# Expert gates: weighted one-hot rows by one compare-and-multiply per token, three of four tokens on GpSimd

## The chip, the cores and the metric

One core of a Trainium2 chip. The metric is the device time of one execution in microseconds (us); smaller is better. All data is fp32.

## The reference

A network of two parts: two layers with feed-forward, Fourier and retention mixers, then two layers (DEPTH = 2) with attention, a recurrent mixer and a product-key expert layer, all for 256 tokens of width 1024. The change lies in the expert layer, which is once in each of the last two layers. It has 128 x 128 experts; each token picks 16 of them in each of 8 heads:

```python
def block(zb):
    q = (zb @ wq).reshape(PEER_TOK_BLOCK, Hp, 2, half)
    s = jnp.einsum('thpd,hpnd->thpn', q, subkeys).astype(jnp.float32)
    s_top, i_top = lax.top_k(s, K)
    cand = (s_top[:, :, 0, :, None] + s_top[:, :, 1, None, :]).reshape(PEER_TOK_BLOCK, Hp, K * K)
    score, flat = lax.top_k(cand, K)
    i1 = jnp.take_along_axis(i_top[:, :, 0], flat // K, axis=-1)
    i2 = jnp.take_along_axis(i_top[:, :, 1], flat % K, axis=-1)
    expert = i1 * PEER_NKEYS + i2
    gate = jax.nn.softmax(score, axis=-1)
    h = jnp.einsum('thkd,td->thk', u_tab[expert], zb).astype(jnp.float32)
    act = (gate * jax.nn.gelu(h, approximate=False)).astype(zb.dtype)
    return jnp.einsum('thk,thkd->td', act, v_tab[expert])
```

The kernel gathers no expert. It runs all of them for all tokens and multiplies by a dense table of gates, which holds for token t the gate at (i1, i2), and zero where an expert wasn't picked.

## The kernel before, in words

**Stages.** The program is a list of stages, and each of the engines (TensorE or PE, VectorE or DVE, ScalarE or ACT, GpSimd or POOL, SyncE or SP) runs its part of them in this order; a stage begins where the semaphore `stage_done` has reached its index. Weights come in blocks of 1 MB through a ring of four (SP issues the loads). ScalarE rounds each block and POOL subtracts the rounded block from the whole one (line 269), so that PE can work with both parts.

**The stage of the gates** is `PeerGates` (lines 2667 to 2731), between `PeerRoute`, which picks the experts, and `PeerExperts`, which runs them. `PeerRoute` leaves in `slot` three rows for each of 256 tokens: i1, i2 and the gate, with the 8 x 16 = 128 picks along the partitions. For one token the gate table of 128 x 128 is then a product over the picks: (one-hot rows of i1, each times its gate) transposed, times (one-hot rows of i2).

- The tokens go in 64 sets (`SETS`) of four (`SET`). `hot` holds four sets (`BUFS`), each with two halves of four 128x128 rows; half 0 is for i1 and half 1 for i2.
- DVE copies iota (0 to 127) into PSUM (line 2693), so that its second input comes from there. For each set it compares iota with i1 and i2 of the four tokens in one instruction of 1024 elements (line 2698) and signals `hot_ready`. From the fifth set on it waits for `done` of the set four before.
- POOL waits for `hot_ready` and multiplies half 0 by the gates in place, 512 elements (line 2707), then signals `weighted`.
- PE waits for `weighted` and, from the fourth set on, for `kept` of the set three before, then does four products of 128x128 (line 2717), two records each, into one of three PSUM banks, and signals `done`.
- ScalarE copies each bank of 512 to the table (line 2728) and signals `kept`. After the last it ends the stage (line 2731).

**Around it.** At the stage's start ScalarE may round blocks that the experts need (line 2723) and waits for earlier stores (line 2724). POOL's queue goes from the last set straight into `PeerExperts.pool`, which makes the remainders of its first blocks (line 269), and DVE's into line 2918. The experts on PE begin at line 2797. The order on each engine is that of the program text; there is no planner.

Of the kernel before, what the change touches and what calls it, by code (L numbers as in the profile page):

```python
# [11 lines left out]
ALU = mybir.AluOpType  # L12
AX = mybir.AxisListType

P = 128
# [63 lines left out]
def columns(table, name, layer=0, width=None):  # L79
    a, b = VEC[name]  # L80
    if width is None:
        return table[:, a:b]
    return table[:, a + layer * width:a + (layer + 1) * width]
# [18 lines left out]
class Share:  # L102
# [3 lines left out]
    def at(self, k):  # L106

        return self.base + k
# [80 lines left out]
class Stage:  # L189
# [82 lines left out]
    def pe(self, pe):  # L272
        pass
# [4 lines left out]
    def dve(self, dve, link):  # L278
        pass
# [62 lines left out]
class Modulation:  # L342
# [5 lines left out]
    TILE = 32  # L348
    SETS = 4
    LATER = 2  # L350
# [43 lines left out]
    def block(self, pe, i):  # L394
# [9 lines left out]
        for e in range(steps):  # L404
            k = steps * (i - 8 * n) + e
            for g in range(self.SETS):
                at = (e * self.SETS + g) * width
                last = mm(c.ps[g * self.TILE:(g + 1) * self.TILE, self.BANK + n % 2, 0:width], self.cond[:, k, :],  # L408
# [25 lines left out]
    def add(self, dve, link, n):  # L434
# [4 lines left out]
        m = self.mods[:].rearrange("p j d s -> p (j d) s")[:, 16 * n:16 * n + 4 * tiles, :].rearrange("p (g m) s -> p g m s", m=tiles)  # L439
        turned = c.ps[:, self.TURNED, 32 * n:32 * n + 8 * tiles].rearrange("p (m g s) -> p g m s", g=self.SETS, s=2)  # L440
        b = columns(c.vec, "b_mod", self.layer, 72)[:, 16 * n:16 * n + 4 * tiles].rearrange("p (g m) -> p g m", m=tiles)
        link(v.tensor_tensor(m, turned, b.unsqueeze(3).broadcast_to([P, self.SETS, tiles, 2]), ALU.add))
        for j in range(2 * n, min(2 * n + 2, N_MOD)):
# [14 lines left out]
class Norm(Stage):  # L458
# [86 lines left out]
    def pe(self, pe):  # L545
# [15 lines left out]
        if self.first_mods:  # L561
# [4 lines left out]
            lead.turn(pe, 0)  # L566

    def dve(self, dve, link):
        c, nc = self.chip, self.nc
        if self.first_mods:  # L570
# [855 lines left out]
class Attention(Stage):  # L1426
# [10 lines left out]
    CMP, SEL, WIN, SWA = range(4)  # L1437
    BUFS = 4
    LEAD = 3
    units = [(t, g, b) for t in range(NT) for g in range(2) for b in range(4)]  # L1440

    def __init__(self, chip, layer, tables):
# [16 lines left out]
        n += 16 + P  # L1459
        assert n + self.BUFS * 8 * 4 <= W_PEND  # L1460
        self.stat = at(n, self.BUFS, 8, 4)
        self.sc = at(B_WORK, self.BUFS, 4, N)
        n = B_WORK + self.BUFS * 4 * N
        self.pt = at(n, 5, 4, P)
# [25 lines left out]
    def pe(self, pe):  # L1490
# [51 lines left out]
        def turn(u):  # L1542
# [5 lines left out]
            for j in range(self.key_tiles(t, b)):  # L1548
                for i in range(4):
                    last = nc.tensor.transpose(ps[0:w, 4 + j, i * P:(i + 1) * P], self.sc[:, u % self.BUFS, i, j * P:j * P + w],  # L1550
                                               self.chip.ident)
# [1115 lines left out]
class PeerGates(Stage):  # L2667
# [4 lines left out]

    SET = 4
    SETS = N // SET
    BUFS = 4
    BANKS = 3

    def __init__(self, chip):
# [5 lines left out]
        self.iota_kept = chip.signals("iota_in_psum", 1)  # L2684
        self.hot_ready = chip.signals("hot_ready", self.SETS)
        self.weighted = chip.signals("weighted", self.SETS)
        self.done = chip.signals("gates_done", self.SETS)
        self.kept = chip.signals("gates_kept", self.SETS)

    def dve(self, dve, link):  # L2690
        v, wide = self.nc.vector, [P, 2, self.SET, P]
        dve.wait_ge(self.chip.stage_done, self.index)
        v.tensor_copy(self.iota, self.chip.iota).then_inc(self.iota_kept.sem, 1)
        dve.wait_ge(self.iota_kept.sem, self.iota_kept.at(1))
        for n in range(self.SETS):
            if n >= self.BUFS:
                dve.wait_ge(self.done.sem, self.done.at(n - self.BUFS + 1))
            v.tensor_tensor(self.hot[:, n % self.BUFS], self.iota.unsqueeze(1).unsqueeze(1).broadcast_to(wide),
                            self.slot[:, 0:2, n * self.SET:(n + 1) * self.SET].unsqueeze(3).broadcast_to(wide),
                            ALU.is_equal).then_inc(self.hot_ready.sem, 1)  # L2700

    def pool(self, pool, link):
        pool.wait_ge(self.chip.stage_done, self.index)
        for n in range(self.SETS):
            hot = self.hot[:, n % self.BUFS, 0]
            pool.wait_ge(self.hot_ready.sem, self.hot_ready.at(n + 1))
            self.nc.gpsimd.tensor_tensor(hot, hot, self.slot[:, 2, n * self.SET:(n + 1) * self.SET].unsqueeze(2)
                                         .broadcast_to([P, self.SET, P]), ALU.mult).then_inc(self.weighted.sem, 1)

    def pe(self, pe):  # L2710
        pe.wait_ge(self.chip.stage_done, self.index)
        for n in range(self.SETS):
            pe.wait_ge(self.weighted.sem, self.weighted.at(n + 1))
            if n >= self.BANKS:
                pe.wait_ge(self.kept.sem, self.kept.at(n - self.BANKS + 1))
            for i in range(self.SET):
                last = self.nc.tensor.matmul(self.chip.ps[:, n % self.BANKS, i * P:(i + 1) * P], self.hot[:, n % self.BUFS, 0, i],  # L2717
                                             self.hot[:, n % self.BUFS, 1, i], start=True, stop=True)
            last.then_inc(self.done.sem, 1)
# [603 lines left out]
```

## Time and profile before

| | |
|---|---|
| median of 3 runs | 4693.72 us (4690.62 to 4700.74) |
| the profiled execution | 4701.88 us |
| its span, first to last instruction | 4700.1 us |
| busy, share of the span | PE 94%, PEld (weight loads) 80%, POOL 56%, ACT 38%, DVE 35% |
| mean granted clock of TensorE | 0.969 |

The stage of the gates runs twice, from about 2560 to 2637 us and from about 3939 to 4015 us. The profile names an instruction by its line, engine and operation, then output<-input with their shapes as partitions x elements; `arena` is the big SBUF buffer that holds `hot`, `slot` and the gates, `ps` is PSUM. Times are of one execution, so a sum is made against the 4701.88 us and then carried to the median.

### The profile page before, as it was taken

The page shows a single profiled execution, that of the slowest core. Times are in us where ns is not written, and L with a number is a line of the kernel's source. Part 1 is how long each engine was busy: PE and PEld are TensorE (multiplying, and loading weights), DVE is VectorE, ACT ScalarE, POOL GpSimd, SP SyncE. Part 2 cuts the span into 40 slices and gives each one's busy share as a digit, 9 for nine tenths or more (in the row PEclk, how much of TensorE's full clock was granted, in tenths as well). Part 3 has the DMA queues.
Part 4 walks back from the last instruction along what each step waited for, and adds up shares of the span by engine and source line. Part 5 has one row for each costly group of instructions (what it writes and reads, how often), then busy time and mean ns, then how long its engine had stood idle before and what let it go on. Part 6 is the DMA issues. An engine that isn't in the chain of part 4 may idle for free.

```text
span 4700.1 us, 62596 instructions
## 1 busy us (share of the span) xinstructions
PE 4437.7 (94%) x24682; PEld 3755.9 (80%) x24682; DVE 1650.6 (35%) x3195; ACT 1806.1 (38%) x2932; POOL 2641.5 (56%) x1282
## 2 busy tenths in 40 slices
PE   7999999999999989889989999999898989999998
PEld 5777777778778879886888888887877888888886
DVE  2211222032010532264468522223454568322223
ACT  3222322132233234434232555555442333555554
POOL 3343243344444357651166888888640366888886
PEclk9999999999999999999999999999999999999999
DMA  6622366222232234440134255555440143355554
GB/s 258 242 106 90 70 247 235 85 90 99 90 107 91 81 117 171 175 171 28 37 144 139 90 187 187 187 187 202 166 153 19 67 143 101 139 187 188 187 187 161
DMA packets 100139, 659.22 MB, mean 140 GB/s; under 512 B 10464, under 2 KB 16864, under 8 KB 22368
## 3 DMA queue, kind: packets, MB, share of 16 engines
q1 hardware_dynamic: 90000, 638.46, 37.6%
q10 hardware_dynamic: 9936, 17.86, 1.4%
q8 instruction: 151, 2.47, 0.2%
q14 instruction: 52, 0.43, 0.0%
HBM read 646.84 MB, written 9.44 MB: 140 GB/s over the span
## 4 chain that ended last, share of the span: by engine, by line
PE 86%; DVE 7%; ACT 2%; POOL 2%; issue 1%; DMA 1%; SPq 0%; ACTq 0%; DVEq 0%; POOLq 0%
PE ps L2807 14%; PE ps L253 14%; PE ps L254 13%; PE ps L255 13%; PE ps L2797 8%; PE ps L2798 4%; PE ps L2717 3%; PE ps L2513 3%; PE ps L1399 2%; POOL ring_rest L269 2%; PE ps L408 1%; PE ps L1569 1%; PE ps L1538 1%; DVE arena L2235 1%; PE ps L1903 1%
## 5 line engine op out<-in xcount | busy, mean ns | idle before, releaser
L269 POOL TENSOR_TENSOR ring_rest<-ring,rounded 128x1024 fp32r<-128x1024 f32 x960 | 2346.4, 2459 | 1489.4 <-ACT rounded L241 1290.8
L253 PE MATMUL ps<-part,rounded 128*128 128x256 f32 (+1 forms) x3456 | 1188.4, 344 | 84.1 <-DVE part L2343 22.4
L254 PE MATMUL ps<-part,rounded 128*128 128x256 f32 (+1 forms) x3456 | 1176.8, 341 | 0.0
L255 PE MATMUL ps<-part,ring_rest 128*128 128x256 f32 (+1 forms) x3456 | 1175.1, 340 | 0.0
L253 PEld LDWEIGHTS ps<-part,rounded 128*128 128x128 f32 x3456 | 670.7, 194 | 186.4 <-issue 26.7
L241 ACT ACTIVATE rounded<-ring 128x1024 fp32r<-128x1024 f32 x496 | 496.4, 1050 | 689.1 <-PE ps L255 679.3
L255 PEld LDWEIGHTS ps<-part,ring_rest 128*128 128x128 f32 x3456 | 670.4, 194 | 69.0
L254 PEld LDWEIGHTS ps<-part,rounded 128*128 128x128 f32 x3456 | 671.3, 194 | 67.4
L2797 PE MATMUL ps<-x_parts,rounded 128*128 128x512 f32 x1728 | 616.9, 397 | 1.5 <-ACTq L2731 1.5
L2896 ACT ACTIVATE rounded<-ring 128x1024 fp32r<-128x1024 f32 x464 | 490.3, 1057 | 329.1 <-DMA ring<-in_weights 327.0
L2807 PE MATMUL ps<-rounded,part 128*128 128x512 f32 x2048 | 592.4, 393 | 16.6 <-POOL ring_rest L269 10.0
L2798 PE MATMUL ps<-x_parts,ring_rest 128*128 128x256 f32 x1728 | 484.7, 280 | 0.0
L2807 PEld LDWEIGHTS ps<-rounded,part 128*128 128x128 f32 x2048 | 368.9, 188 | 99.6 <-POOL ring_rest L269 13.4
L2797 PEld LDWEIGHTS ps<-x_parts,rounded 128*128 128x128 f32 x1728 | 324.6, 188 | 79.4 <-ACTq L2731 1.8
L2798 PEld LDWEIGHTS ps<-x_parts,ring_rest 128*128 128x128 f32 x1728 | 325.9, 189 | 8.3
L2927 DVE TENSOR_TENSOR ps<-ps,arena 128x256 f32<-128x256 f32 x216 | 134.8, 624 | 545.6 <-ACT ps L2864 545.6
L2807 PE MATMUL ps<-ring_rest,part 128*128 128x512 f32 x1024 | 320.6, 395 | 0.0
L686 ACT ACTIVATE arena<-ps 128x512 f32<-128x512 f32 (+1 forms) x88 | 47.9, 544 | 617.8 <-PE ps L255 617.8
L700 DVE TENSOR_TENSOR part<-ps,arena 128x512 f32<-128x512 f32 (+1 forms) x88 | 55.0, 625 | 556.9 <-ACT arena L686 556.9
L2807 PEld LDWEIGHTS ps<-ring_rest,part 128*128 128x128 f32 x1024 | 192.1, 188 | 47.3
L772 DVE SCALAR_TENSOR_TENSOR x<-ps,mods,x 128x256 f32<-128x256 f32 x80 | 35.8, 480 | 507.1 <-PE ps L255 507.1
L2321 POOL TENSOR_TENSOR part<-arena,part 128x1024 fp32r<-128x1024 f32 x6 | 14.5, 2423 | 304.0 <-ACT part L2301 304.0
(362 smaller groups left out, 5374.8 us busy)
## 6 DMA issues: line engine op xcount, KB each, us to landing
ring<-in_weights SPq DMA_DIRECT2D x528, 1024.0 KB, 4.8
arena<-in_mod_weights SPq DMA_DIRECT2D x72, 1024.0 KB, 7.9
held<-arena ACTq DMA_DIRECT2D x20, 256.0 KB, 5.5
arena<-held SPq DMA_DIRECT2D x20, 256.0 KB, 4.5
arena<-bias_scratch ACTq DMA_DIRECT2D x2, 2048.0 KB, 9.9
bias_scratch<-arena ACTq DMA_DIRECT2D x1, 3072.0 KB, 32.1
x<-in_x SPq DMA_DIRECT2D x1, 2048.0 KB, 9.9
arena<-in_keys ACTq DMA_DIRECT2D x2, 1024.0 KB, 4.8
```

The costliest lines, as they stand in the source:

```text
L241: self.nc.scalar.activation(c.rounded[:, s % ROUNDED, half], c.ring[:, slot, half], ACT.Copy)\
L253: mm(out, w[0], a[0], start=start, stop=False)
L254: mm(out, w[0], a[1], start=False, stop=False)
L255: return mm(out, w[1], a[0], start=False, stop=stop)
L269: eng.tensor_tensor(c.ring_rest[:, slot, half], c.ring[:, slot, half], c.rounded[:, (self.s0 + r) % ROUNDED, half].bitcast(F32), ALU.subtr ...
L2513: last = nc.tensor.matmul(ps[:, 4 + u % self.AHEAD_BANKS, 0:N], self.chip.ring[:, slot, e * KD + k, :], self.z_whole[:, k, :], start=k == ...
L2717: last = self.nc.tensor.matmul(self.chip.ps[:, n % self.BANKS, i * P:(i + 1) * P], self.hot[:, n % self.BUFS, 0, i], self.hot[:, n % self. ...
L2797: nc.tensor.matmul(c.ps[:, r % 2, :], whi[:, k, :], c.x_parts[:, k, :], start=k == 0, stop=False)
L2798: last = nc.tensor.matmul(c.ps[:, r % 2, 0:N], wlo[:, k, :], self.z[0][:, k, :], start=False, stop=k == KD - 1)
L2807: last = nc.tensor.matmul(self.out(t, i), a, w[:, i * 4 * P:(i + 1) * 4 * P], start=False, stop=end and n == 2)
L2896: self.nc.scalar.activation(c.rounded[:, (self.s0 + r) % ROUNDED, half], c.ring[:, f % RING, half], ACT.Copy)\
L2927: v.tensor_tensor(gelu, gelu, self.gates[:, :, bass.ds(b + HELD, 1)].rearrange("p t a -> p (t a)"), ALU.mult)\
```

## The change

The multiplication by the gate and the comparison with i1 become one instruction per token: `tensor_scalar` with iota as its input and two column operands (one value per partition each), i1 for `is_equal` and the gate for `mult`. POOL does it for three tokens of each set (`OWN`), reading iota from SBUF, and no longer waits for DVE; from the fifth set on it waits for `done` as DVE does. DVE compares i2 for all four tokens (512 elements) and does the fused instruction for the fourth token, reading iota from PSUM. PE waits for both.

```diff
@@ -2672,6 +2672,7 @@
 
     SET = 4
     SETS = N // SET
+    OWN = 3
     BUFS = 4
     BANKS = 3
 
@@ -2687,29 +2688,38 @@
         self.done = chip.signals("gates_done", self.SETS)
         self.kept = chip.signals("gates_kept", self.SETS)
 
+    def weigh(self, eng, iota, n, i):
+        token = n * self.SET + i
+        return eng.tensor_scalar(self.hot[:, n % self.BUFS, 0, i], iota, self.slot[:, 0, token:token + 1],
+                                 self.slot[:, 2, token:token + 1], ALU.is_equal, ALU.mult)
+
     def dve(self, dve, link):
-        v, wide = self.nc.vector, [P, 2, self.SET, P]
+        v, wide = self.nc.vector, [P, self.SET, P]
         dve.wait_ge(self.chip.stage_done, self.index)
         v.tensor_copy(self.iota, self.chip.iota).then_inc(self.iota_kept.sem, 1)
         dve.wait_ge(self.iota_kept.sem, self.iota_kept.at(1))
         for n in range(self.SETS):
             if n >= self.BUFS:
                 dve.wait_ge(self.done.sem, self.done.at(n - self.BUFS + 1))
-            v.tensor_tensor(self.hot[:, n % self.BUFS], self.iota.unsqueeze(1).unsqueeze(1).broadcast_to(wide),
-                            self.slot[:, 0:2, n * self.SET:(n + 1) * self.SET].unsqueeze(3).broadcast_to(wide),
-                            ALU.is_equal).then_inc(self.hot_ready.sem, 1)
+            v.tensor_tensor(self.hot[:, n % self.BUFS, 1], self.iota.unsqueeze(1).broadcast_to(wide),
+                            self.slot[:, 1, n * self.SET:(n + 1) * self.SET].unsqueeze(2).broadcast_to(wide), ALU.is_equal)
+            for i in range(self.OWN, self.SET):
+                last = self.weigh(v, self.iota, n, i)
+            last.then_inc(self.hot_ready.sem, 1)
 
     def pool(self, pool, link):
         pool.wait_ge(self.chip.stage_done, self.index)
         for n in range(self.SETS):
-            hot = self.hot[:, n % self.BUFS, 0]
-            pool.wait_ge(self.hot_ready.sem, self.hot_ready.at(n + 1))
-            self.nc.gpsimd.tensor_tensor(hot, hot, self.slot[:, 2, n * self.SET:(n + 1) * self.SET].unsqueeze(2)
-                                         .broadcast_to([P, self.SET, P]), ALU.mult).then_inc(self.weighted.sem, 1)
+            if n >= self.BUFS:
+                pool.wait_ge(self.done.sem, self.done.at(n - self.BUFS + 1))
+            for i in range(self.OWN):
+                last = self.weigh(self.nc.gpsimd, self.chip.iota, n, i)
+            last.then_inc(self.weighted.sem, 1)
 
     def pe(self, pe):
         pe.wait_ge(self.chip.stage_done, self.index)
         for n in range(self.SETS):
+            pe.wait_ge(self.hot_ready.sem, self.hot_ready.at(n + 1))
             pe.wait_ge(self.weighted.sem, self.weighted.at(n + 1))
             if n >= self.BANKS:
                 pe.wait_ge(self.kept.sem, self.kept.at(n - self.BANKS + 1))
```

## Rows read from the trace of the kernel before

**Rows 1.** The page, part 4: the chain that ended last

```profile
PE ps L2807 14%; PE ps L253 14%; PE ps L254 13%; PE ps L255 13%; PE ps L2797 8%; PE ps L2798 4%; PE ps L2717 3%; PE ps L2513 3%; PE ps L1399 2%; POOL ring_rest L269 2%; PE ps L408 1%; PE ps L1569 1%; PE ps L1538 1%; DVE arena L2235 1%; PE ps L1903 1%
```

**Rows 2.** The chain of waits, 2555 to 2650 us; start us, us, what

```profile
2559.66 0.31 DVE ps L2693
2559.99 1.24 DVE arena L2698
...
2561.36 1.05 POOL arena L2707
...
2562.54 73.72 PE ps L2717 x512
2636.28 0.61 ACT arena L2728
2636.98 0.50 PE ps L2797
```

**Rows 3.** Lines from 2574 to 2635 us: busy us, mean ns, idle before

```profile
L2717 PE MATMUL ps<-arena 128*128 128x128 f32 x433 | 61.4, 288 | 0.0
L2698 DVE TENSOR_TENSOR arena<-ps,arena 128x1024 f32<-128x1024 f32 x53 | 60.0, 1210 | 0.0
L2707 POOL TENSOR_TENSOR arena<-arena 128x512 f32<-128x512 f32 x54 | 56.2, 1041 | 4.9
L2717 PEld LDWEIGHTS ps<-arena 128*128 128x128 f32 x432 | 52.3, 191 | 8.8 <-POOL arena L2707 8.8
```

**Rows 4.** Timeline from 2568 us; start us, us, engine line, [idle before, releaser]

```profile
2568.04 8.18 DVE L2698 TENSOR_TENSOR arena<-ps,arena 128x1024 f32<-128x1024 f32 x7 [0.48 <-PE ps L2717]
...
2570.24 0.60 ACT L2728 ACTIVATE arena<-ps 128x512 f32<-128x512 f32 x1 [0.30 <-PE ps L2717]
...
2571.13 0.60 ACT L2728 ACTIVATE arena<-ps 128x512 f32<-128x512 f32 x1 [0.30 <-PE ps L2717]
2572.02 0.60 ACT L2728 ACTIVATE arena<-ps 128x512 f32<-128x512 f32 x1 [0.30 <-PE ps L2717]
...
2574.00 0.97 PEld L2717 LDWEIGHTS ps<-arena 128*128 128x128 f32 x8 [0.16 <-POOL arena L2707]
```

**Rows 5.** Windows by engine, core 0; fifth pair of columns POOL, then PEclk

```profile
2562.50:2568.00 5.50, 5.46 (x25) 5.49 (x26) 4.55 (x4) 1.19 (x2) 4.45 (x5) 0.50 0.00 0
...
2574.00:2635.00 61.00, 61.00 (x433) 52.25 (x432) 59.91 (x53) 32.27 (x54) 56.20 (x55) 1.00 0.01 1
```

**Rows 6.** L2698 over both layers; duration min/median/max ns, first and last start

```profile
L2698 DVE TENSOR_TENSOR arena<-ps,arena x128: 1210/1210/1225, 2560.0 to 4010.5; 128x1024 f32<-128x1024 f32 x128
```

**Rows 7.** Lines by form, engine DVE: one input, none to two column operands

```profile
L2134 DVE TENSOR_SCALAR arena<-arena,vec 128x128 f32<-128x128 f32 x16 | 4.5, 342 | 0.1
...
L2124 DVE TENSOR_SCALAR arena<-ps 128x512 f32<-128x512 f32 x4 | 2.8, 691 | 15.0 <-PE ps L1855 14.9
...
L1837 DVE TENSOR_SCALAR x<-arena,vec 128x256 f32<-128x256 f32 x8 | 2.3, 349 | 0.1
...
L2071 DVE TENSOR_SCALAR arena<-arena 128x1024 f32<-128x1024 f32 x2 | 1.4, 694 | 18.1 <-ACT arena L1990 18.1
```

**Rows 8.** Timeline of DVE at 2308 us: four of those back to back

```profile
2308.78 1.11 DVE L2134 TENSOR_SCALAR arena<-arena,vec 128x128 f32<-128x128 f32 x4
```

**Rows 9.** Lines by form, engine POOL, whole span

```profile
L1720 POOL TENSOR_TENSOR arena<-arena 128x1024 f32<-128x1024 f32 x12 | 22.7, 1894 | 40.1 <-DVE arena L1704 38.7 <-DVE arena L1699 1.4
...
L1720 POOL TENSOR_TENSOR arena<-arena 128x512 f32<-128x512 f32 x12 | 12.5, 1041 | 34.0 <-DVE arena L1704 23.2 <-DVE arena L1699 10.8
...
L2584 POOL TENSOR_TENSOR arena<-arena 128x32 f32<-128x32 f32 x32 | 7.1, 243 | 1.3
L2580 POOL TENSOR_TENSOR arena<-arena 128x128 f32<-128x128 f32 x16 | 6.4, 401 | 1.3
```

**Rows 10.** Timeline of POOL near 3920 us: two instructions back to back

```profile
3924.75 0.44 POOL L2584 TENSOR_TENSOR arena<-arena 128x32 f32<-128x32 f32 x2
```

**Rows 11.** L2614: min/median/max ns of one form

```profile
L2614 DVE TENSOR_TENSOR arena<-arena x16: 268/268/2483, 2450.2 to 3908.8; 128x112 f32<-128x112 f32 x16
```

## The prediction

> **What bounds the kernel now.** I read the page's chain first, to see what the touched code can be worth. TensorE carries the run, and the one-hot products of line 2717 hold 3% of the chain, some 150 us in two layers [rows 1]. So only this stage moves, and the rest of the 4.7 ms stays as it is. The chain of waits through the first layer's stage puts it in order: DVE copies iota at 2559.66, compares set 0, GpSimd multiplies it, and from 2562.54 the chain stays on PE for 73.72 us until ScalarE's last copy; 0.09 us after that copy the experts begin at 2636.98 [rows 2]. A chain on PE isn't yet a stage bound by PE, so the next views ask who paces it.
>
> In the middle of the stage DVE is busy for 60.0 us in 53 comparisons with no idle time, that is 1.132 us a set (the single instruction reads 1210 ns; neighbours overlap by 78). POOL has 4.9 us of idle time in 54 sets. PE's weight loads stand 8.8 us waiting for POOL, about 0.16 us in every set [rows 3]. PE shows as fully busy only because its ends are modelled. DVE is the pace, POOL (1.04 us a set) comes right behind it, PE behind both. How fast PE would go is seen where it eats sets that were made ahead: ScalarE's copies then start at 2570.24, 2571.13 and 2572.02, 0.89 us apart, and the weight loads wait for POOL again at 2574.00 [rows 4]. Earlier, from 2562.5 to 2568, PE has granted clock 0.50 (1.2 GHz) after its pause, and later 1.00 (2.4 GHz) [rows 5]; in that slow stretch PE is the bound whatever the makers do. In layer 1 DVE works without a break from 2568.04, with 58 of 64 sets to come [rows 4]; in layer 2 it is free of the slow stretch sooner and goes at its own pace for all 64 [rows 6]. So 122 sets are paced by the maker.
>
> **The change, part by part.** The new pace P is the slowest of three: DVE, POOL, PE.
>
> DVE loses half of its comparison: 512 elements in place of 1024. A one-input operation on 512 elements from PSUM takes 691 ns [rows 7], against 1210 for the 1024 [rows 3]: 519 ns less (1.014 ns an element), so the cadence is 1.132 - 0.519 = 0.61 us. It gains one compare-and-multiply of 128 elements from PSUM with two column operands. The nearest row is line 2134: two column operands, 128 elements, 342 ns, and four of them in 1.11 us, so one every (1.11 - 0.342)/3 = 0.256 us [rows 7, 8]. That row reads SBUF, where 1024 elements cost (694 ns) what 512 cost from PSUM (691): half the price per element. From PSUM it is 128 x 0.507 = 0.065 us more, 0.32 us. DVE: 0.61 + 0.32 = 0.93 us.
>
> POOL loses a 128x512 product (1041 ns) and gains three compare-and-multiplies of 128x128 a set, 384 in both layers. No POOL row shows that operation, so its price is the unknown of this change. POOL's two-input rows lie on a line: (1894 - 1041)/512 = 1.67 ns an element and 188 ns fixed, which gives 401 for 128 elements, as measured [rows 9]. Two of them back to back take 0.44 us where one takes 0.243, so 46 ns of each is hidden [rows 10]. The new one has one input in place of two: at best 0.83 ns an element, 107 ns; at worst the rate stays, 213 ns. It also fetches two columns. On DVE the rows without, with one and with two of them have fixed parts of 694 - 519 = 175, 349 - 130 = 219 and 342 - 65 = 277 ns [rows 7]: 44 for one, 102 for both. For POOL the ends are then 188 + 107 = 295 ns (columns free) and 188 + 213 + 102 = 503 ns. I take the halved element price, since it is the second stream that goes, and 73 ns for the columns, between one fetch and two: 368 ns, 322 in a row. Three are 0.97 us.
>
> The GPSIMD Engine Reference of the Trainium skill (section 4.1) calls one-input operations on GpSimd roughly line-rate, which agrees with the halved slope; no POOL row here shows one. The same page (section 7) says that a loop that produces a truth value costs about 2.03 cycles an element unless it is unrolled, and that each small read command costs about 102 cycles. By estimates from these the operation would be near 295 ns or near 570 ns, which is P at 0.93 or at 1.57, and the stage faster than DVE's old pace or much slower.
>
> PE keeps its products and gets a second wait a set: 0.89 us and at most the 0.16 us of its present handover again, 1.05 [rows 4]. I take it as hidden: both makers run ahead of it and the 0.97 of POOL covers 0.08 us. ScalarE's copies follow PE as before.
>
> So P = 0.97, and the steady part gains 122 x (1.132 - 0.97) = 19.8 us.
>
> The ends: POOL no longer stands behind DVE. The first product could start at 2559.66 + 0.33 + 0.61 + 0.32 + 0.08 + 0.13 = 2561.1 in place of 2562.54 [rows 2]: 1.4 us. At the end a product of 1.04 us with its handover is off the chain: 1.2 us. In layer 1 both count (makers and PE are tied together in the slow stretch), in layer 2 the makers' chain is one piece and 1.5 us is left: 4.1 us. Against it: some operations of DVE now and then take some 2.2 us more than their kind, as line 2614 with 268 ns at the median and 2483 at most [rows 11]. A new form at the start can meet that on either engine: 0 to 2.2 us a layer, taken as 1: 2 us. The buffers, of which there are still four, the waits for free ones and the queues of SP and ScalarE are unchanged. POOL's next work, two remainders of the first expert block, starts when its last set is done, and so moves with the stage.
>
> Sum: 19.8 + 4.1 - 2 = 21.9 us. The profiled execution took 4701.9 us, so 4680 by its own time; the median of the three runs is 4693.7, 0.17% lower, and the forecast against it is 4672.
>
> One more way to lose: DVE and GpSimd share a way into SBUF. The rows show no such loss (POOL's product reads 1041 ns in line 1720 and beside DVE's comparisons alike [rows 3, 9]). SBUF — State Buffer of the Trainium skill ("Who interferes with whom") says that a `tensor_scalar` in a two-port mode shuts GpSimd out for its whole length; were it so, POOL's pace would be 0.97 + 0.32 = 1.29. Its condition is a source in SBUF, and the copy of iota in PSUM stays the source on DVE, so I leave this out of the sum and give it 0.02 of the chance of slower.
>
> **The rivals.** With POOL's operation at d ns, P = 3(d - 46), and the whole changes sign at P = 1.149, d = 429.
>
> *Slower, POOL becomes the bound.* The element price doesn't fall: d = 188 + 213 + 73 = 474, P = 1.28, 122 x (-0.15) + 2 = -16 us, 4710; with both columns at full price d = 503, P = 1.37, -29 us with the 2.2 us starts, 4723. Dearer still, if each column took half of POOL's fixed 188 ns: d = 589, P = 1.63, -59 us, 4752; this is where the skill's two costs of section 7 point, and it has 0.08 of the 0.32. For it: three fixed parts of 188 ns stand in place of one, 0.42 us a set more, and POOL was already at 92% of its pace. Against it: one stream goes.
>
> *No change.* d between 403 and 455, P 1.07 to 1.23: the plain two-input row of 401 ns is at the edge of it. 4684 to 4703.
>
> *All of it is realised.* d up to 356: DVE at 0.93 is the bound, with PE right behind. 122 x 0.20 + 4.1 = 28.7 us without the start cost: 4665. This is the better end of my own case. If the second wait costs PE its full 0.16, P = 1.05 and the gain 12 us, 4682, still my case.
>
> **How the numbers follow.** A change under 0.2% (9.4 us) can't be told from none. My case, d below 403 ns, runs from 4665 to 4684 and gets 0.52 (0.22 of it at the DVE bound); no change 0.16; slower 0.32. The range takes in the best end with 2 us of play, 4663, and the slower case up to 4723 with as much play as the runs before show (7 us), 4730; the dearer 0.08 is left out, with some 0.05 below.
>
> **What would show it.** In the profile after: three POOL TENSOR_SCALAR rows a set, 128x128, near 368 ns (right: under 403; wrong: over 455); DVE's comparison near 691 ns and its small one near 400; POOL without idle time in the stage, PE's weight loads waiting for POOL; ScalarE's copies 0.97 us apart; the stage about 63 us long instead of 74. If they are 0.93 apart and wait for DVE, the better end holds; over 1.15 apart, the forecast is wrong and POOL's price is the step that failed. A wait of PE that ends with neither maker would say that its second wait costs.

## The result, and the profile after

The changed kernel takes 4852.1 us (median of 4 runs, 4849.5 to 4854.5) against 4696.6 us before: ratio 1.033, 95% interval 1.0315 to 1.0346. It is some 155 us slower, where a gain of 22 us was forecast and 4730 was the upper end.

The page of the changed kernel, cut to its span, its busy times and the clock in 40 slices:

```profile
span 4847.7 us, 62984 instructions
...
PE 4504.4 (93%) x24682; PEld 3813.2 (79%) x24682; DVE 1636.7 (34%) x3323; ACT 1805.3 (37%) x2932; POOL 2803.4 (58%) x1538
...
PEclk9999999999999999999997899999999997899999
```

POOL has 162 us more busy time than before. The clock row has two dips, in the 22nd and 23rd and in the 34th and 35th of its 40 slices; they hold the two stages of the gates. The new operation over the whole run, on both engines (duration min/median/max in ns):

```profile
L2693 POOL TENSOR_SCALAR arena<-cst,arena x384: 790/834/875, 2556.0 to 4155.1; 128x128 f32<-128x128 f32 x192
L2693 DVE TENSOR_SCALAR arena<-ps,arena x128: 399/402/405, 2556.9 to 4148.6; 128x128 f32<-128x128 f32 x128
```

DVE, with iota in PSUM, does it in 402 ns and GpSimd, with iota in SBUF, in 834. The groups in the middle of the stage, which answer to [rows 3] (busy us, mean ns, idle before):

```profile
L2693 POOL TENSOR_SCALAR arena<-cst,arena 128x128 f32<-128x128 f32 x150 | 116.1, 829 | 0.0
L2727 PE MATMUL ps<-arena 128*128 128x128 f32 x400 | 80.9, 366 | 35.1 <-DVE arena L2693 23.8 <-issue 11.2
L2727 PEld LDWEIGHTS ps<-arena 128*128 128x128 f32 x399 | 70.2, 265 | 45.0 <-DVE arena L2693 27.1 <-issue 17.9
L2704 DVE TENSOR_TENSOR arena<-ps,arena 128x512 f32<-128x512 f32 x50 | 34.6, 692 | 64.7 <-PE ps L2727 64.7
L2738 ACT ACTIVATE arena<-ps 128x512 f32<-128x512 f32 x50 | 29.9, 597 | 85.3 <-PE ps L2727 85.3
L2693 DVE TENSOR_SCALAR arena<-ps,arena 128x128 f32<-128x128 f32 x50 | 20.1, 402 | 0.0
```

POOL has no idle time at all in 115 us. Before, it was idle 4.9 us in 61. DVE, the pace before, now waits 64.7 us for TensorE's `done`, and ScalarE 85.3 us. This reads as one engine that paces everybody. The timeline of the same stretch shows one period, of 2.32 us:

```profile
2599.32 13.19 POOL L2693 TENSOR_SCALAR arena<-cst,arena 128x128 f32<-128x128 f32 x17
...
2600.24 2.05 PE L2727 MATMUL ps<-arena 128*128 128x128 f32 x8 [1.19 <-DVE arena L2693]
2602.32 0.60 ACT L2738 ACTIVATE arena<-ps 128x512 f32<-128x512 f32 x1 [2.64 <-PE ps L2727]
2602.32 0.69 DVE L2704 TENSOR_TENSOR arena<-ps,arena 128x512 f32<-128x512 f32 x1 [2.23 <-PE ps L2727]
...
2604.64 0.60 ACT L2738 ACTIVATE arena<-ps 128x512 f32<-128x512 f32 x1 [1.72 <-PE ps L2727]
```

POOL does 17 operations in 13.19 us without a gap. The releaser that PE names here is DVE's small operation, and the groups above name it too. The start of the stage shows that this is not what PE waited for, and it has the prices of DVE's two operations back to back:

```profile
2557.56 23.23 POOL L2693 TENSOR_SCALAR arena<-cst,arena 128x128 f32<-128x128 f32 x30
...
2558.11 0.68 DVE L2704 TENSOR_TENSOR arena<-ps,arena 128x512 f32<-128x512 f32 x1
...
2558.50 2.04 PE L2727 MATMUL ps<-arena 128*128 128x128 f32 x8 [3.06 <-POOL arena L2693]
2558.71 0.40 DVE L2693 TENSOR_SCALAR arena<-ps,arena 128x128 f32<-128x128 f32 x1
2559.03 0.68 DVE L2704 TENSOR_TENSOR arena<-ps,arena 128x512 f32<-128x512 f32 x1
2559.62 0.41 DVE L2693 TENSOR_SCALAR arena<-ps,arena 128x128 f32<-128x128 f32 x1
...
2564.91 0.40 DVE L2693 TENSOR_SCALAR arena<-ps,arena 128x128 f32<-128x128 f32 x1
...
2565.41 1.78 PE L2727 MATMUL ps<-arena 128*128 128x128 f32 x8 [1.15 <-DVE arena L2693]
```

POOL's 30 operations take 23.23 us: 0.774 us from one start to the next, 2.32 a set. PE's row at 2565.41 is the fourth set. DVE had made its rows for that set by 2560.03 (the pair at 2559.03 and 2559.62); the operation at 2564.91, which the profile names, is for the seventh. POOL's twelfth operation, the last of the fourth set, ends near 2556.01 + 12 x 0.774 = 2565.30, and PE starts 0.11 us later. DVE runs three sets ahead, ScalarE and DVE wait for PE, PE waits for POOL, and POOL never waits.

From 2558.11 to 2558.71 and on to 2559.03 are 0.60 and 0.32 us, together 0.92 where 0.93 was forecast. DVE's copy of iota, with which the stage starts, begins at 2555.94 in this run, and the first product comes 2.56 us later, where it took 2.88 before [rows 2].

### The profile page after: what moved, and what is told of

Read it like the earlier page. It is cut to its first block, busy times and chain, and to the rows that moved or that the text cites. A ratio compares the mean times of both kernels' runs of the same rounds, so it can differ in the third digit from the quotient of the medians.

```text
span 4847.7 us, 62984 instructions
## 1 busy us (share of the span) xinstructions
PE 4504.4 (93%) x24682; PEld 3813.2 (79%) x24682; DVE 1636.7 (34%) x3323; ACT 1805.3 (37%) x2932; POOL 2803.4 (58%) x1538
## 4 chain that ended last, share of the span: by engine, by line
PE 85%; DVE 8%; ACT 2%; issue 2%; POOL 2%; DMA 1%; SPq 0%; ACTq 0%; DVEq 0%; POOLq 0%
PE ps L2817 14%; PE ps L253 13%; PE ps L254 13%; PE ps L255 13%; PE ps L2807 8%; PE ps L2727 4%; PE ps L2808 4%; PE ps L2513 3%; PE ps L1399 2%; POOL ring_rest L269 2%; PE ps L408 1%; PE ps L1538 1%; PE ps L1569 1%; DVE arena L2235 1%; PE ps L1903 1%
## 5 line engine op out<-in xcount | busy, mean ns | idle before, releaser
L2693 POOL TENSOR_SCALAR arena<-cst,arena 128x128 f32<-128x128 f32 x384 | 297.1, 830 | 19.3 <-ACTq L2565 19.3
L2727 PE MATMUL ps<-arena 128*128 128x128 f32 x1024 | 213.4, 374 | 89.2 <-DVE arena L2693 52.4
L2727 PEld LDWEIGHTS ps<-arena 128*128 128x128 f32 x1024 | 186.0, 273 | 116.8 <-DVE arena L2693 59.5
```

The lines of the kernel that those rows point to most:

```text
L2693: return eng.tensor_scalar(self.hot[:, n % self.BUFS, 0, i], iota, self.slot[:, 0, token:token + 1], self.slot[:, 2, token:token + 1], ALU ...
```

## The experiments

All were made from the changed kernel by editing GpSimd's operation alone, if nothing else is said. "In a row" is the time from one start to the next, read from a timeline row as its length over its count. The total of the kernel before, in the same jobs, was between 4690 and 4702 us. Every version but the last was run once, so the readings rest on the traces more than on the totals.

### One column in place of two

```diff
@@ -2692,0 +2693,3 @@
+        if eng is self.nc.gpsimd:
+            return eng.tensor_scalar(self.hot[:, n % self.BUFS, 0, i], iota, self.slot[:, 0, token:token + 1],
+                                     1.0, ALU.is_equal, ALU.mult)
```

> On GpSimd the gate's column is replaced by the constant 1.0 (so the gate is left out for three of four tokens); all else as in the changed kernel, where one operation costs 0.774 us in a row. Theory F (the fetches of the two columns are the price): one fetch gone, (0.774 - 0.25)/2 = 0.26 us less an operation, pace 2.32 -> about 1.54 us a set, total about 4752. Theory E (the price is per element, in the loop) and theory C (the comparison takes a slow path): no change, pace 2.32, about 4852.

Measured 4817.4 us, between the two. POOL in the timeline from 2575 us:

```profile
2574.75 15.29 POOL L2694 TENSOR_SCALAR arena<-cst,arena 128x128 f32<-128x128 f32 x22
```

15.29/22 = 0.695 us in a row. The column is worth 0.08 us, not 0.26: theory F falls as the main cause.

### No column

```diff
@@ -2692,0 +2693,2 @@
+        if eng is self.nc.gpsimd:
+            return eng.tensor_scalar(self.hot[:, n % self.BUFS, 0, i], iota, 5.0, 1.0, ALU.is_equal, ALU.mult)
```

> Both columns on GpSimd are constants (5.0 and 1.0; the one-hot rows of three of four tokens are left out of the computation). Theory F: the operation falls to about 0.25 us in a row, POOL is no longer the bound, DVE's pace of 0.93 holds, about 4670. Theories E and C: pace 2.32, about 4852.

Measured 4818.4 us, nearer to theories E and C. POOL's group from 2575 to 2650 us:

```profile
L2694 POOL TENSOR_SCALAR arena<-cst 128x128 f32<-128x128 f32 x106 | 68.1, 642 | 7.2
```

The operation itself is shorter again (642 ns against 721 with one column), but POOL now has 7.2 us of idle time over 106 operations with no releaser named, and the time from one to the next is (68.1 + 7.2)/106 = 0.71 us, no better than with one column. So with both columns gone nine tenths of the price are still there.

### No comparison

```diff
@@ -2692,0 +2693,3 @@
+        if eng is self.nc.gpsimd:
+            return eng.tensor_scalar(self.hot[:, n % self.BUFS, 0, i], iota, self.slot[:, 0, token:token + 1],
+                                     self.slot[:, 2, token:token + 1], ALU.mult, ALU.mult)
```

> On GpSimd the comparison is replaced by a multiplication, with both columns kept (the one-hot of three of four tokens is left out). Theory C: the operation loses its slow path and falls to 0.25 to 0.37 us in a row, pace 0.93 to 1.1, total 4670 to 4690. Theories F and E: no change, pace 2.32, about 4852.

Measured 4712.0 us, 22 us above the upper end of theory C and 140 below the others. POOL in the timeline from 2575 us:

```profile
2574.91 15.43 POOL L2694 TENSOR_SCALAR arena<-cst,arena 128x128 f32<-128x128 f32 x36
```

15.43/36 = 0.429 us in a row, 0.345 less than with the comparison, where theory C had 0.25 to 0.37 us. Both columns, the second multiplication, the input and the places are the same; only the first operation differs. It is the comparison.

### Two halves

```diff
@@ -2692,0 +2693,6 @@
+        if eng is self.nc.gpsimd:
+            for h in range(0, P, P // 2):
+                last = eng.tensor_scalar(self.hot[:, n % self.BUFS, 0, i, h:h + P // 2], iota[:, h:h + P // 2],
+                                         self.slot[:, 0, token:token + 1], self.slot[:, 2, token:token + 1],
+                                         ALU.is_equal, ALU.mult)
+            return last
```

> Each of GpSimd's operations is made as two, of 64 elements each: six in place of three a set, the same elements. Theory F (a fixed price, paid per instruction): 0.72 us each, pace about 4.3, total about 5105. Theory E (188 ns fixed less 46 hidden, the rest 4.9 ns an element): 0.14 + 64 x 0.0049 = 0.46 us each, pace 2.75, total about 4907. Theory C as E, if the slow path is in the loop.

Measured 4978.1 us, between the two, so neither was right as it stood. POOL in the timeline from 2575 us:

```profile
2574.46 16.08 POOL L2695 TENSOR_SCALAR arena<-cst,arena 128x64 f32<-128x64 f32 x29
```

16.08/29 = 0.555 us for 64 elements against 0.774 for 128: 3.42 ns an element, and 0.336 us that does not depend on them, if the two lengths lie on a straight line; no third length was tried.

### Only the comparison

```diff
@@ -2692,0 +2693,3 @@
+        if eng is self.nc.gpsimd:
+            return eng.tensor_scalar(self.hot[:, n % self.BUFS, 0, i], iota, self.slot[:, 0, token:token + 1],
+                                     None, ALU.is_equal)
```

> GpSimd only compares: one column and one stage of arithmetic, no multiplication (the gate is left out for three of four tokens). The runs so far: both columns and comparison 0.774 us in a row, one column and a constant about 0.70, two columns with a multiplication in place of the comparison 0.43. Theory K (a comparison costs about 2.7 ns an element more in GpSimd's loop, wherever it stands): about 0.65 to 0.70 us, pace 2.0 to 2.1, total 4800 to 4817. Rival S (it is the comparison's result fed to a second stage that is slow): 0.33 to 0.40 us, pace about 1.1, total 4690 to 4710.

Measured 4771.8 us, between the theories, nearer to K. POOL in the timeline from 2575 us:

```profile
2574.66 15.61 POOL L2694 TENSOR_SCALAR arena<-cst,arena 128x128 f32<-128x128 f32 x27
```

15.61/27 = 0.578 us. Without any second stage the comparison is still 0.15 us dearer than two multiplications with two columns. The second stage with its constant is worth 0.12 of the 0.695; rival S, by which the second stage makes the whole difference, falls. A lone multiplication was not run, so how the 0.345 us would come out without a second stage is not known.

### Two tokens for GpSimd, two for DVE

```diff
@@ -2675 +2675 @@
-    OWN = 3
+    OWN = 2
```

> GpSimd weighs two of four tokens, DVE the other two. If the stage is simply paced by the slower maker: POOL 2 x 0.774 = 1.55 us a set, DVE 0.61 + 2 x 0.32 = 1.25; 128 x 0.774 = 99 us less than the changed kernel and a few more for the clock that TensorE gets back, about 4748. Rival (DVE and GpSimd stand in each other's way once both are busy): POOL's operation above 0.8 us in a row, total above 4760.

Measured 4746.5 us against 4748 expected. POOL in the timeline from 2575 us:

```profile
2574.91 15.49 POOL L2693 TENSOR_SCALAR arena<-cst,arena 128x128 f32<-128x128 f32 x20
```

15.49/20 = 0.775 us, unchanged while DVE, which has the other two tokens, is idle for only 6.2 of 45 us. The two engines don't hold each other up here, and the count of operations times 0.774 is the pace.

### Each product twice

```diff
@@ -2727,2 +2727,3 @@
-                last = self.nc.tensor.matmul(self.chip.ps[:, n % self.BANKS, i * P:(i + 1) * P], self.hot[:, n % self.BUFS, 0, i],
-                                             self.hot[:, n % self.BUFS, 1, i], start=True, stop=True)
+                for again in range(2):
+                    last = self.nc.tensor.matmul(self.chip.ps[:, n % self.BANKS, i * P:(i + 1) * P], self.hot[:, n % self.BUFS, 0, i],
+                                                 self.hot[:, n % self.BUFS, 1, i], start=True, stop=True)
```

> The changed kernel with each of TensorE's gate products made twice over into the same place, so that it works through its idle time (the same result). POOL's pace of 2.32 us stays. Theory G (of the 156 us, POOL's pace explains 148 and the rest is the clock: TensorE is granted 0.74 on average in the stage, and the experts' first products run at 1.2 GHz): clock near 1.00 in the stage, the first expert block in about 3.1 us in place of 5.4, total 4845 to 4849, 4 to 6 us less. Rival (the rest has another source): as the changed kernel, 4850 to 4855, with the experts' start as slow as now.

Measured 4848.8 us, inside the band of theory G, but one run is too coarse for 4 us, so the trace has to tell. First the windows from 2575 to 2690 us, of the changed kernel and then of this one (columns as in [rows 5]: PE, PEld, DVE, ACT, POOL; the clock is the third number from the end):

```profile
2575.00:2690.00 115.00, 80.21 (x400) 70.03 (x399) 49.95 (x100) 29.32 (x50) 115.00 (x150) 0.74 0.00 1
```

```profile
2575.00:2690.00 115.00, 100.14 (x793) 92.07 (x793) 50.48 (x100) 29.85 (x50) 115.00 (x150) 1.00 0.00 1
```

PE's granted clock is 0.74 on average (between its levels of 1.2 and 2.4 GHz) where it idles 35.1 of 115 us (the groups of the changed kernel), and 1.00 where it makes each product twice. With two tokens for each engine it paused in each set too, 12.1 of 45 us, and was granted 1.00. Then the chain of waits at the end of the stage, from ScalarE's last copy over the experts' first products to ScalarE's first copy of their result. The changed kernel:

```profile
2706.77 0.61 ACT arena L2738
...
2712.90 0.39 ACT arena L2871
```

With each product twice:

```profile
2709.90 0.61 ACT arena L2739
...
2713.78 0.39 ACT arena L2872
```

From the last copy to the experts' first result are 6.13 us in the changed kernel, where those products start at the slow clock, and 3.88 us here: 2.25 us in layer 1. In layer 2 the changed kernel needs less:

```profile
4158.20 0.60 ACT L2738 ACTIVATE arena<-ps 128x512 f32<-128x512 f32 x1 [1.72 <-PE ps L2727]
4163.97 0.39 ACT L2871 ACTIVATE arena<-ps 128x256 f32<-128x256 f32 x1 [5.18 <-PE ps L2808]
```

These are 5.77 us, against 3.88 here (4160.10 to 4163.98). So 2.25 and 1.89, together 4.1 us, is what the clock cost behind the two stages. The kernel before has its last copy at 2636.28 [rows 2] and the experts' first result 3.88 us later too:

```profile
2640.16 0.39 ACT L2861 ACTIVATE arena<-ps 128x256 f32<-128x256 f32 x1 [3.28 <-PE ps L2798]
```

The stage itself is as long at the one clock as at the other, as POOL is the bound: the last copy of gates comes 150.76 us after POOL's first operation in the changed kernel (2556.01 to 2706.77) and 150.66 here (2559.24 to 2709.90). But this run doesn't tell what the slow clock costs in the very last set, which comes after POOL's last operation: PE's eight records take 2.06 us there in the changed kernel, and the sixteen of the doubled products 2.04 here. In other sets of the changed kernel eight records take 1.13 us (at 2700.04), so by an estimate up to 0.9 us a layer of the 150.76 can be the clock's.

### Greater-or-equal in place of equal

```diff
@@ -2692,0 +2693,3 @@
+        if eng is self.nc.gpsimd:
+            return eng.tensor_scalar(self.hot[:, n % self.BUFS, 0, i], iota, self.slot[:, 0, token:token + 1],
+                                     self.slot[:, 2, token:token + 1], ALU.is_ge, ALU.mult)
```

> The changed kernel with greater-or-equal in place of equal on GpSimd (three of four tokens' one-hot rows become steps). Theory K (every comparison costs about 2.7 ns an element more): 0.774 us in a row, total about 4850. Rival Q (equality alone is slow): 0.43 us, pace 1.28, total about 4712.

Measured 4851.9 us. POOL in the timeline from 2575 us:

```profile
2574.69 15.55 POOL L2694 TENSOR_SCALAR arena<-cst,arena 128x128 f32<-128x128 f32 x20
```

15.55/20 = 0.778 us, as with equality: theory K.

### Halves without the comparison

```diff
@@ -2692,0 +2693,6 @@
+        if eng is self.nc.gpsimd:
+            for h in range(0, P, P // 2):
+                last = eng.tensor_scalar(self.hot[:, n % self.BUFS, 0, i, h:h + P // 2], iota[:, h:h + P // 2],
+                                         self.slot[:, 0, token:token + 1], self.slot[:, 2, token:token + 1],
+                                         ALU.mult, ALU.mult)
+            return last
```

> On GpSimd multiplication in place of comparison (the one-hot of three of four tokens left out), in two instructions of 64 elements each. With the comparison the halves cost 0.555 and the whole 0.774 us in a row: 3.42 ns an element and 0.336 fixed. If the comparison's price lies in the loop, the fixed part is the same here and the element costs (0.428 - 0.336)/128 = 0.72 ns: 0.382 us each, pace 2.29, total about 4845. If part of the price is per instruction, the fixed part is smaller here: 0.30 to 0.33 us each, pace 1.8 to 2.0, total 4780 to 4810.

Measured 4834.1 us, between the two expectations. POOL in the timeline from 2575 us:

```profile
2574.63 15.51 POOL L2695 TENSOR_SCALAR arena<-cst,arena 128x64 f32<-128x64 f32 x42
```

15.51/42 = 0.369 us for 64 elements, against 0.429 for 128: 0.93 ns an element and 0.31 fixed. Beside 3.42 and 0.336 with the comparison: of the 0.345 us, 128 x 2.49 = 0.32 go with the elements and 0.026 are fixed. Here too a straight line through two lengths is taken for granted.

### Fewer comparisons: the outer product

GpSimd's comparison is dear, and DVE's costs by its width, so a version was made that leaves GpSimd none and DVE narrower ones. The diff, much cut, is against the kernel before. i1 = 8 x high + low; a one-hot row of 128 is the outer product of one of 16 and one of 8.

```diff
-            v.tensor_tensor(self.hot[:, n % self.BUFS], self.iota.unsqueeze(1).unsqueeze(1).broadcast_to(wide),
-                            self.slot[:, 0:2, n * self.SET:(n + 1) * self.SET].unsqueeze(3).broadcast_to(wide),
-                            ALU.is_equal).then_inc(self.hot_ready.sem, 1)
...
+            v.tensor_tensor(cols, self.iota[:, 0:self.COLS].unsqueeze(1).broadcast_to(wc),
+                            self.slot[:, 0, some].unsqueeze(2).broadcast_to(wc), ALU.is_equal)
+            link(v.tensor_tensor(rows, self.iota[:, 0:self.ROWS].unsqueeze(1).broadcast_to(wr),
+                                 self.row[:, some].unsqueeze(2).broadcast_to(wr), ALU.is_equal))
+            link(v.tensor_tensor(cols, cols, self.slot[:, 2, some].unsqueeze(2).broadcast_to(wc), ALU.mult))
...
+            last = v.tensor_tensor(self.hot[:, n % self.BUFS, 1], self.iota.unsqueeze(1).broadcast_to(wide),
+                                   self.slot[:, 1, n * self.SET:(n + 1) * self.SET].unsqueeze(2).broadcast_to(wide), ALU.is_equal)
...
+        return eng.tensor_tensor(self.hot[:, n % self.BUFS, 0, tokens].rearrange("p i (a c) -> p i a c", c=self.COLS),
+                                 self.rows[:, b, some].unsqueeze(3).broadcast_to(wide),
+                                 self.cols[:, b, some].unsqueeze(2).broadcast_to(wide), ALU.mult)
```

`slot[0]` holds the low part here and `row` the high one; `some` is 16 tokens in the first three operations, the tokens of the set in the last.

> A version without comparisons on GpSimd and with fewer on DVE: i1 is cut into its eighth and its rest (in each stage's first three small DVE operations), and DVE compares 16 and 8 numbers a token in place of 128, for 16 tokens at a time, and multiplies the 8 by the gate; the weighted row is the product of the 16 and the 8, a two-input multiplication, done by GpSimd for four or three tokens and by DVE for the odd sets' fourth. Three buffers in place of four. POOL: 0.995 and 0.78 us by turns, 0.89 on average; DVE: 0.61 + 0.25 + 0.11 = 0.97; TensorE 0.89. If these add as they stand: pace 0.97, 122 x 0.16 = 20 us less than before and 3 us of prologue back, about 4677. Rival (DVE's operations with two SBUF inputs and GpSimd's hold each other up, or GpSimd pays for short inner rows as in its 722 ns for 256 elements): pace 1.1 or more, no gain, 4690 or above.

Measured 4696.5 us: no gain, the rival. (With 2^23 as its rounding constant the rows for i1 of 0 and 1 are left out; the work done is the same.) DVE's groups from 2575 to 2620 us:

```profile
L2728 DVE TENSOR_TENSOR arena<-arena 128x128 f32<-128x128 f32 x10 | 8.2, 820 | 0.3
L2698 DVE TENSOR_TENSOR arena<-arena 128x128 f32<-128x128 f32 x21 | 7.5, 358 | 0.0
L2726 DVE TENSOR_TENSOR arena<-ps,arena 128x256 f32<-128x256 f32 x10 | 4.1, 409 | 0.0
```

The multiplication of 128 elements by the gates (line 2728), with both inputs in SBUF, takes 820 ns, and a comparison of 256 elements with one input in PSUM (line 2726) 409. The timeline shows one batch of four sets:

```profile
2591.13 0.28 DVE L2724 TENSOR_TENSOR arena<-ps,arena 128x128 f32<-128x128 f32 x1
...
2591.78 0.82 DVE L2728 TENSOR_TENSOR arena<-arena 128x128 f32<-128x128 f32 x1
...
2595.59 0.28 DVE L2724 TENSOR_TENSOR arena<-ps,arena 128x128 f32<-128x128 f32 x1
```

From 2591.13 to 2595.59 are 4.46 us, 1.115 a set, with DVE idle for 0.7 of the 45 us. The start of the stage in the same trace has the same instruction before POOL's first product and beside it:

```profile
2562.10 0.29 DVE L2728 TENSOR_TENSOR arena<-arena 128x128 f32<-128x128 f32 x1
...
2563.26 3.06 POOL L2698 TENSOR_TENSOR arena<-arena 128x512 f32<-128x512 f32 x3 [12.85 <-DVE arena L2737]
2563.68 0.80 DVE L2728 TENSOR_TENSOR arena<-arena 128x128 f32<-128x128 f32 x1
```

It takes 0.29 us while POOL is idle and 0.80 while POOL works. Not every operation with two SBUF inputs pays so much: DVE's own products of 128 (line 2698) take 358 ns on average in the same 45 us.

The next version (the diff is against the one just shown) takes the second SBUF input from every DVE operation, keeps four tokens for GpSimd in three sets of four, and mends the constant:

```diff
-            v.tensor_tensor(cols, self.iota[:, 0:self.COLS].unsqueeze(1).broadcast_to(wc),
-                            self.slot[:, 0, some].unsqueeze(2).broadcast_to(wc), ALU.is_equal)
+            v.tensor_tensor(self.near, self.iota[:, 0:self.COLS].unsqueeze(1).broadcast_to(wc),
+                            self.low[:, some].unsqueeze(2).broadcast_to(wc), ALU.is_equal)
...
-            link(v.tensor_tensor(cols, cols, self.slot[:, 2, some].unsqueeze(2).broadcast_to(wc), ALU.mult))
+            v.tensor_tensor(cols, self.near, self.slot[:, 2, some].unsqueeze(2).broadcast_to(wc), ALU.mult)
...
-                last = self.outer(v, n, slice(self.mine(n), self.SET))
+                last = v.tensor_scalar(self.hot[:, n % self.BUFS, 0, i], self.iota, self.slot[:, 0, token:token + 1],
+                                       self.slot[:, 2, token:token + 1], ALU.is_equal, ALU.mult)
```

`near` lies in PSUM, as does the high part; the comparison of 16 reads the high part from there and iota from SBUF.

> As the version before it, but with the rounding constant mended (1.5 x 2^23), the eighths kept in PSUM and the compare of 8 written to PSUM, so that no DVE operation has two SBUF inputs, and the fourth token of every fourth set made by DVE in one compare-and-multiply with iota from PSUM. DVE: 0.61 + (0.20 + 0.45 + 0.33)/4 + 0.32/4 = 0.94 us a set; POOL 3 x 1.00 + 0.78 over 4 = 0.95; TensorE 0.89. Theory M (the 0.82 us of DVE's small multiplication in the run before was the wait for GpSimd at their shared way, 0.29 without): pace 0.95, 122 x 0.18 = 22 us less than before, 2 us of prologue back, ratio 0.9957. Rival (the loss has another source and comes back): DVE's small operations long again, pace 1.1, ratio 0.999 to 1.000.

Measured 4684.2 us (median of 8) against 4697.4: ratio 0.9974, interval 0.9964 to 0.9985. It is 13 us faster than the kernel before, a quarter of a percent and clear of the interval, and so faster than both kernels. Its groups from 2575 to 2620 us, and the timeline of one batch:

```profile
L2699 POOL TENSOR_TENSOR arena<-arena 128x512 f32<-128x512 f32 x36 | 37.4, 1067 | 0.0
L2738 DVE TENSOR_TENSOR arena<-ps,arena 128x512 f32<-128x512 f32 x47 | 31.2, 686 | 1.5
...
L2699 POOL TENSOR_TENSOR arena<-arena 128x384 f32<-128x384 f32 x12 | 10.2, 848 | 0.0
```

```profile
2590.10 0.60 ACT L2774 ACTIVATE arena<-ps 128x512 f32<-128x512 f32 x1 [0.43 <-PE ps L2763]
...
2591.13 0.60 ACT L2774 ACTIVATE arena<-ps 128x512 f32<-128x512 f32 x1 [0.43 <-PE ps L2763]
2591.36 0.29 DVE L2729 TENSOR_TENSOR arena<-ps,arena 128x128 f32<-128x128 f32 x1
...
2592.02 0.60 ACT L2774 ACTIVATE arena<-ps 128x512 f32<-128x512 f32 x1 [0.30 <-PE ps L2763]
...
2593.99 0.60 ACT L2774 ACTIVATE arena<-ps 128x512 f32<-128x512 f32 x1 [0.43 <-PE ps L2763]
```

The small multiplication takes 0.29 us in place of 0.82, so theory M holds. ScalarE's copies at 2590.10 and 2593.99 are four sets apart: 0.973 us a set, near the 0.95 expected, with POOL never idle and DVE for 1.5 of 45 us. The gain of 13 us is 7 short of the expected 20. The pace accounts for 2.6 of them (122 x (1.132 - 0.973) = 19.4 in place of 22), and the prologue for some 1.5 more: DVE's copy of iota begins at 2558.58 here and PE's first product at 2563.20, 4.62 us against 2.88 before [rows 2]. Where the rest lies is not known.

## Why the prediction was wrong, point by point

**What bounds the stage** was read rightly: DVE at 1.132 us a set, POOL behind it, PE at 0.89. PE's price is confirmed by the last version, whose copies at 2591.13 and 2592.02 are 0.89 apart although PE has two waits a set; in this pair the second wait costs nothing to be seen.

**DVE's share** was right: 0.61 + 0.32 = 0.93 forecast, 0.60 + 0.32 measured.

**POOL's operation is the step that failed.** "I take the halved element price, since it is the second stream that goes, and 73 ns for the columns": 368 ns, 322 in a row. It takes 834, 774 in a row, so 2.32 us a set in place of 0.97, and the slower rival's dearest form had 589. In the terms of that sum, in a row:

| term | forecast | measured |
|---|---|---|
| fixed, with the columns, less what is hidden | 188 + 73 - 46 = 215 ns | 310 ns |
| 128 elements, one input, no comparison | 107 ns | 119 ns (0.93 each) |
| the comparison | nothing | 345 ns (2.49 an element, 26 fixed) |
| sum | 322 ns | 774 ns |

The halving was nearly right. The fixed part was 95 ns too small: the second column alone costs 79 (0.774 less 0.695), where 73 stood for both, and the second stage of arithmetic with a constant costs 117 (0.695 less 0.578, how much of it fixed is not known) and had no term. The DVE rows from which the columns' price came have one stage with no column or with one, and two stages with two, so they could not separate these. What was absent is the comparison: the sum drew the price from rows whose arithmetic is a multiplication or a sum, and the argument named inputs and columns but never asked whether another operation costs the same. On DVE it does (692 ns for the comparison of 512 in the changed kernel, 691 for the multiplication and sum of line 2124 [rows 7]). Why a comparison takes GpSimd longer is not shown.

The GPSIMD Engine Reference of the Trainium skill (section 7) has a rule that pointed the right way, 2.03 cycles an element for a loop that makes a truth value, by an estimate with the 1.2 GHz of its section 1 some 1.7 ns; the forecast gave the two costs of that section 0.08. The measured 3.42 ns is twice that.

The trace of before had a warning. The line of 1.67 ns an element went through the cheapest of POOL's rows; others of the same shapes are dearer than the 1041 and 1894 ns of [rows 9]:

```profile
L269 POOL TENSOR_TENSOR ring_rest<-ring,rounded 128x1024 fp32r<-128x1024 f32 x960 | 2346.4, 2459 | 1489.4 <-ACT rounded L241 1290.8 <-ACT rounded L2896 194.2
...
L2580 POOL TENSOR_TENSOR arena<-arena 128x512 f32<-128x512 f32 x16 | 20.2, 1263 | 1.3
```

The first is a subtraction and the second a sum, where line 1720 multiplies by a broadcast value. So shape and count of inputs alone didn't fix a price on GpSimd; which of the differences does was not tried.

**The rival** "POOL becomes the bound" was right in its mechanism and too small in its price. Its formula P = 3(d - 46) gives 3 x (834 - 46) = 2.36 against 2.32 measured. Its dearest total was 4752 us, 100 below what came.

**The ends.** 1.4 us were expected at the head; it was 0.3 (2.88 less 2.56), since POOL's three operations are what the first product waits for. The 2 us for first uses of a new form that take 2.2 us more than their kind did not show: POOL's 384 operations lie between 790 and 875 ns and DVE's 128 between 399 and 405. What the end of the stage gave can't be read off here, since PE's last eight records ran at the slow clock.

**What the sum makes of it.** The stage, from DVE's copy of iota to ScalarE's last copy, grew from 76.62 us (2559.66 to 2636.28) to 150.83 (2555.94 to 2706.77) in layer 1 and from 75.50 (3938.59 to 4014.09) to 150.83 (4007.37 to 4158.20) in layer 2: 149.5 us. The clock behind the stages adds 4.1. That is 153.7, beside 155.5 between the medians. The two profiled executions lie only 147.6 us apart (spans of 4700.1 and 4847.7), since the changed kernel's ran 6.1 us shorter outside these stretches. Of that, 3.7 us lie before the first stage of the gates, where the two kernels are the same; the runs of the kernel before differ by 10 us among themselves.

**The shared way into SBUF** was left out of the sum for this change, rightly: with DVE's iota in PSUM POOL keeps 0.775 us when DVE is busy for 38.9 of 45 us. It came back in the outer product, where one operation of DVE with two SBUF inputs took 820 ns beside POOL's product and 290 without. SBUF — State Buffer of the Trainium skill ("Who interferes with whom") says that a DVE instruction with two SBUF inputs contends with a GpSimd instruction that reads SBUF, and this agrees.

## What to carry to other kernels

Price an operation on GpSimd from a row of GpSimd with the same arithmetic, not only with the same shape: here a comparison costs 3.42 ns an element and a multiplication 0.93. Where no such row exists, the dearest neighbour is no bound: this operation came out at 834 ns, where the sum's dearest end was 503. Such an unknown belongs in the range, or is measured first. Where a one-hot row is needed, cut the index: comparisons of 16 and 8 and a multiplication take the place of 128 comparisons, and GpSimd does that multiplication for four tokens in 1.07 us. When the profile names a releaser, check by the program's order that the operation named makes what the waiting one needs.

## What the runs showed of the hardware that was not expected

- A comparison in GpSimd's `tensor_scalar` costs 3.42 ns an element, a multiplication 0.93; equal and greater-or-equal are alike (0.774 and 0.778 us in a row for 128).
- With two constants in place of columns POOL's operation is shorter (642 against 721 ns) and yet the next one comes no earlier, 0.71 us after it, with a gap that the profile names nobody for. Why was not tried.
- TensorE, idle for 35.1 of 115 us, was granted 0.74 on average in the stage, and began the experts at the slow level: 2.25 us in one layer and 1.89 in the other. Making each product twice kept the clock at 1.00.
- A multiplication on DVE with two SBUF inputs took 0.29 us while GpSimd was idle and 0.80 beside GpSimd's product.
